# Attention steps in pairs in a two-layer gMLP and differential-attention trunk on one Trainium2 core

## What is computed

```
h  = rms_norm(x, pre_mix_g[l]);  z = h @ w_in[l]          # 1024 -> 2560: u | v | q | k | values
# A: gMLP: layer_norm(gelu(v)), per 128-position block and channel group W_s @ v + b, times gelu(u)
# B: differential attention, 4 heads, blocks of 128 queries, chunk mask:
s  = einsum('bqhjd,bkhjd->jbhqk', q, k)                    # j = 0, 1, 64 channels each
p  = softmax(where(mask, s, -1e30));  a = p[0] - lam * p[1]
o  = einsum('bhqk,bkhe->bqhe', a, v);  o = rms_norm(o, subln_g) * (1 - lam_init)
x  = x + rms_norm(concat(A, B) @ w_out[l], post_mix_g[l])
x  = x + rms_norm(swiglu(rms_norm(x, pre_ffn_g[l])), post_ffn_g[l])
```

## Time and profile before

| | us |
|---|---|
| median of 3 runs | 1099.1 |
| lowest and highest | 1099.06, 1099.11 |
| the profiled execution | 1099.09 |
| its span, first to last instruction | 1097.3 |
| PE busy | 1088.6 |
| DVE, ACT, POOL busy | 585.7, 578.5, 573.4 |

### The profile page before, as it was taken

One profiled execution on the slowest core, in us unless ns is written; L12 is line 12 of the kernel. 1 busy time (PEld: TensorE's weight loads), 2 busy tenths in 40 slices (PEclk: granted clock), 3 DMA queues, 4 the chain that ended last, 5 costly groups with the idle time before them and its releaser, 6 DMA issues.

```text
span 1097.3 us, 17449 instructions
## 1 busy us (share of the span) xinstructions
PE 1088.6 (99%) x6776; PEld 964.2 (88%) x6776; DVE 585.7 (53%) x994; ACT 578.5 (53%) x1135; POOL 573.4 (52%) x450
## 2 busy tenths in 40 slices
PE   8999999999999999999999999999999999999998
PEld 7777778999999999888887787789999999998886
DVE  4353535888888885010254445548888888820103
ACT  5656584566555554221456557756565555531212
POOL 3524254666666665544444324645776666655440
PEclk9999999999999999999999999999999999999999
DMA  8423213414334334622243221133333433353212
GB/s 278 135 58 96 67 50 96 154 57 129 94 108 116 100 95 154 210 96 96 77 136 120 77 72 64 60 95 129 101 114 95 116 114 92 105 211 116 97 57 77
DMA packets 144791, 118.33 MB, mean 108 GB/s; under 512 B 3754, under 2 KB 120004, under 8 KB 144708
## 3 DMA queue, kind: packets, MB, share of 16 engines
q1 hardware_dynamic: 144692, 117.20, 34.2%
q10 hardware_dynamic: 16, 0.00, 0.0%
HBM read 110.90 MB, written 6.29 MB: 107 GB/s over the span
## 4 chain that ended last, share of the span: by engine, by line
PE 97%; ACT 1%; DVE 1%; DMA 0%; issue 0%; DVEq 0%; ACTq 0%
PE banks L596 30%; PE banks L598 30%; PE banks L597 29%; PE banks L655 2%; PE banks L685 2%; PE banks L605 1%; PE banks L670 1%; PE banks L699 1%; PE banks L865 1%; DMA v_att<-in_pre_mix_g_dram 0%; PE banks L706 0%; ACT swap L1218 0%; PE banks L844 0%; PE banks L951 0%; ACT junk L1085 0%
## 5 line engine op out<-in xcount | busy, mean ns | idle before, releaser
L527 POOL TENSOR_TENSOR w_lo<-raw,w_hi 128x512 fp32r<-128x512 f32 x204 | 259.7, 1297 | 302.6 <-ACT w_hi L1077 302.6
L545 POOL TENSOR_TENSOR w_lo<-raw,w_hi 128x512 fp32r<-128x512 f32 x200 | 260.0, 1311 | 142.8 <-ACT w_hi L1146 138.3
L596 PE MATMUL banks<-xg_hi,w_hi 128*128 128x256 f32 (+1 forms) x896 | 278.1, 310 | 0.1
L598 PE MATMUL banks<-xg_lo,w_hi 128*128 128x256 f32 (+1 forms) x896 | 274.4, 306 | 0.0
L597 PE MATMUL banks<-xg_hi,w_lo 128*128 128x256 f32 (+1 forms) x896 | 274.0, 306 | 0.0
L1077 ACT ACTIVATE w_hi<-raw 128x1024 fp32r<-128x1024 f32 x102 | 106.9, 1056 | 170.8 <-PE banks L598 155.0
L1146 ACT ACTIVATE w_hi<-raw 128x512 fp32r<-128x512 f32 x200 | 124.9, 630 | 112.0 <-DVE raw L1761 60.7
L596 PEld LDWEIGHTS banks<-xg_hi,w_hi 128*128 128x128 f32 x896 | 171.2, 191 | 10.8 <-issue 3.3
L598 PEld LDWEIGHTS banks<-xg_lo,w_hi 128*128 128x128 f32 x896 | 171.2, 191 | 8.1
L597 PEld LDWEIGHTS banks<-xg_hi,w_lo 128*128 128x128 f32 x896 | 171.3, 191 | 6.6
L596 PE MATMUL banks<-w_hi,hid_hi 128*128 128x512 f32 x352 | 137.2, 390 | 0.0
(11 more groups left out here) (173 smaller groups left out, 1789.8 us busy)
## 6 DMA issues: line engine op xcount, KB each, us to landing
raw<-in_w_gate_up_dram SPq DMA_DIRECT2D x88, 512.0 KB, 4.1
raw<-in_w_down_dram SPq DMA_DIRECT2D x44, 512.0 KB, 3.5
raw<-in_w_in_dram SPq DMA_DIRECT2D x40, 512.0 KB, 3.8
raw<-in_w_out_dram SPq DMA_DIRECT2D x16, 512.0 KB, 3.5
x_spill<-x_rows SPq DMA_DIRECT2D x8, 512.0 KB, 5.3
x_rows<-x_spill SPq DMA_DIRECT2D x8, 512.0 KB, 5.1
x_rows<-in_x_dram SPq DMA_DIRECT2D x4, 512.0 KB, 6.8
out_dram<-x_rows SPq DMA_DIRECT2D x8, 256.0 KB, 2.0
```

The source lines that it names most:

```text
L527: last = tt(lo[:, piece], raw_half(l, c, h)[:, piece], hi[:, piece].bitcast(F32), ALU.subtract)
L545: tt(lo, full, hi.bitcast(F32), ALU.subtract).then_inc(w_ready, 1)
L596: mm(o, stat[0], mov[0], start=first, stop=False)
L598: return mm(o, stat[0], mov[1], start=False, stop=last)
```

## The change

The order of the attention part is written anew on PE, ACT and DVE.

- Scores are made two steps at a time (`scores_of_two`), without a projection between them. Maxima and combinations follow in pairs as well.
- A head's first two turned tiles go into one bank: step n % 4 = 0 at tile 0, step n % 4 = 1 at tiles 1 and 2. The second turn no longer waits for a copy of the first, and one copy of 384 columns takes both. There are 12 copies in a layer and no longer 16.
- The four gates stand in a row, in banks 2 to 5, which are the scores' banks (`GATE_BANKS`). Scores 8 and 9 wait for them to be read.
- At the start of the program the first norm's gain is loaded into rows that nothing clears, so that its DMA waits for nothing, and DVE copies it into place. Row 3 of x is normalized on DVE before the low part of row 2 is made; ACT makes the high part of row 2 after the root of row 3.

No large product is added or left out. The core of the diff:

```
+                elif n == 8 or n == 9:
+                    pe.wait_ge(gm_added, G * l + 2 * (n - 7))            # in scores
...
-                elif n == 6:
-                    pe.wait_ge(gm_added, G * l + 1)
-                elif n == 8:
-                    pe.wait_ge(gm_added, G * l + 4)
-                else:
+                elif n % ST != 1:
                     pe.wait_ge(at_copied, NS * l + n)                    # in turn
+                at = 1 if n % ST == 1 else 0
                 for k in range(n % ST + 1):
-                    last = tr(b_tr[T_BANK][:, k, :], attn[n % 2][:, k * P:(k + 1) * P], ident[:, :])
+                    last = tr(b_tr[T_BANK][:, at + k, :], attn[n % 2][:, k * P:(k + 1) * P], ident[:, :])
...
+                pe.wait_ge(a_ready, NS * l + (7 if g < 2 else 8))        # in gate
+                    last = mm(b_tr[GATE_BANKS[g]][:, n, :], v_gate[:, n, g * P:(g + 1) * P], wsT[:, g, :],
...
-            act.wait_ge(gain0_zero, 1)
-            act.dma_start(gain0_rows[0:KT, :], pre_mix_g[0].rearrange("(k p) -> k p", k=KT)).then_inc(gain0_landed, 16)
+            act.dma_start(gain0_in, pre_mix_g[0].rearrange("(k p) -> k p", k=KT)).then_inc(gain0_landed, 16)
...
+            copy(gain0_rows[0:KT, :], gain0_in).then_inc(gain0_placed, 1)
...
             norm_row(0, 2)
+            norm_row(0, 3)
             xg_low(0, 2)
-            norm_row(0, 3)
             xg_low(0, 3)
```

More of the change, by code:

```diff
@@ L954, in _ @@
+                turn_two(4)
                 weigh(l, 0)
                 va(C_VA + 1, 1, (2, 3))
-                turn(l, 4)
                 qk_half(l, 4, lower)
-                scores(l, 6)
-                turn(l, 5)
+                turn(l, 6)
                 weigh(l, 1)
                 qk_half(l, 4, upper)
-                scores(l, 7)
-                gate(l, 0)
+                turn(l, 7)
+                weigh(l, 2)
                 qk_half(l, 5, lower)
-                turn(l, 6)
-                weigh(l, 2)
@@ L967, in _ @@
                 qk_half(l, 5, upper)
-                turn(l, 7)
+                for g in range(G):
+                    gate(l, g)
+                weigh(l, 3)
                 qk_half(l, 6, lower)
-                gate(l, 1)
                 qk_half(l, 6, upper)
-                scores(l, 8)
-                gate(l, 2)
-                weigh(l, 3)
+                scores_of_two(8)
                 qk_half(l, 7, lower)
-                scores(l, 9)
-                gate(l, 3)
                 qk_half(l, 7, upper)
+                scores_of_two(10)
@@ L979, in _ @@
+                turn_two(8)
                 u_half(l, 0, lower)
-                turn(l, 8)
-                scores(l, 10)
                 u_half(l, 0, upper)
-                turn(l, 9)
-                scores(l, 11)
-                u_half(l, 1, lower)
                 turn(l, 10)
                 weigh(l, 4)
-                scores(l, 12)
+                u_half(l, 1, lower)
+                turn(l, 11)
+                scores_of_two(12)
                 u_half(l, 1, upper)
-                scores(l, 13)
@@ L991, in _ @@
-                turn(l, 11)
                 u_half(l, 2, lower)
-                turn(l, 12)
+                scores_of_two(14)
+                turn_two(12)
                 weigh(l, 5)
                 u_half(l, 2, upper)
-                scores(l, 14)
-                turn(l, 13)
                 u_half(l, 3, lower)
-                scores(l, 15)
+                turn(l, 14)
                 weigh(l, 6)
                 u_half(l, 3, upper)
-                turn(l, 14)
+                turn(l, 15)
@@ L1003, in _ @@
                 out_k(l, 0)
-                turn(l, 15)
                 out_k(l, 1)
@@ L1236, in copy_turned @@
                         act.wait_ge(pv_ready, 8 * l + (n - 4) // 2 + 1)
-                    w = (n % ST + 1) * P
-                    fn(attnT[:, AT_AT[n % ST]:AT_AT[n % ST] + w], bank[T_BANK][:, 0:w], ACT.Copy)\
-                        .then_inc(at_copied, 1)
+                    if n % ST == 1:
+                        fn(attnT[:, 0:3 * P], bank[T_BANK][:, 0:3 * P], ACT.Copy).then_inc(at_copied, 2)
+                    else:
+                        w = (n % ST + 1) * P
+                        fn(attnT[:, AT_AT[n % ST]:AT_AT[n % ST] + w], bank[T_BANK][:, 0:w], ACT.Copy)\
+                            .then_inc(at_copied, 1)
                 def take_heads(m):
@@ L1652, in _ @@
                     dve.wait_ge(par_ready, 1 + 2 * L)
-                maxima(0)
                 dve.wait_ge(ln_root_ready, l + 1)
```

140 lines of the change are left out of this document (68 added, 72 removed).

## The result

The changed kernel takes **1089.9 us** (median of 4 runs, 1089.69 to 1090.42) where the kernel before takes 1099.08 (4 runs, 1099.01 to 1099.11). The ratio is 0.9918, with a 95% interval from 0.9906 to 0.9929: 9.2 us are gone. The prediction was 1095.2, with a range from 1094.3 to 1096.8. The direction was right; the gain is more than twice what was predicted and lies outside the range.

What follows compares the result with a forecast made beforehand. PE was taken to bound the kernel. Savings of 2.9 (score pairs), 0.5 (row 3), 0.3 (rotation of q) and 0.2 (gain's DMA) sum to 3.9 us: 1099.1 to 1095.2 us, range 1094.3 to 1096.8.

Steps and rivals of the forecast that it cites:

- What bounds the kernel: Whole kernel: PE is 97% of the chain, so only its start-to-start distances and few waits count.
- Eight entries and exits a layer: Attention scores: pairing leaves eight entries and exits where 16 were, saving 1.47 us a layer, 2.9 us in two.
- Failed step 1: Joint between a pair's two scores: the second score follows like a second pass, at no extra cost.
- the other end: Eight joints of scores: each costs 0.1 us less than nothing, 1.5 us more in all; named but not taken.
- I count the rest as zero: Attention's turns and gates: fewer copies and fewer borders between fp32 and projections, beyond the scores' own, save nothing.
- Failed step 2: Program start: the gain's DMA goes some 0.3 us earlier, worth 0.2 us; bounds 0.2 lost to 0.8 gained.
- Row 3 and the rotation of q: PE's waits before row 3's turning and before layer 0's first scores go, saving 0.5 and 0.3 us.
- The covers: Attention handoffs: no new PE waits; closest are scores 10 and 11, cover 1.0 to 1.2 us, and out_k(2), 0.2.
- Joints at full or half cost: Rivals at score joints: a second score pays entry and exit fully, 1098.1 us (chance 0.06), or half, 1096.7 (0.03).
- the late end: Rival at the attention's end: ACT's chain late, PE waits 0.5 us in each layer, 1096.2 us; chance 0.11.
- starved scores: Rival in the attention: bursts from pairs make PE wait at four places a layer, 8 us lost, 1103.2; chance 0.03.

Runs made afterwards that it cites:

- the run of the pairs alone: The changed kernel with both start edits (gain's DMA and row 3) undone, leaving only the new attention order: 1091.91 us, ratio 0.9937 to the kernel before.
- the late gain: The kernel before with the gain's DMA into its own rows and DVE's copy, but its issue again waiting for the clearing: 1099.43 us, ratio 1.0003.

## Why the prediction was wrong, point by point

**What bounds the kernel: right.** PE is 98% of the chain, and everything gained was gained in its distances and gaps.

**Eight entries and exits a layer: right in kind and size.** Entry is 0.32 against 0.23 (0.31 at the pair shown) and the first step behind a pair 0.34, once per pair. This part was the predicted 1.47 us a layer.

**Failed step 1: "A score's second pass is to its first what a second score is to the first, so I take no extra cost".** A second score costs less than a first. A score's keys cost 0.213 us for 128, and 0.21 more is paid once at the ends of a run of scores, however many scores are in it (1, 2 or 4 in the runs). The two passes of a lone score carry 0.1 each of it, being the first and the last; I took that spare distance for part of the work of every pass. The prediction even named the other end, 0.1 us less at each joint, and dropped it as something "which nothing in the rows supports"; the rows did support it, and twice as much. The prediction itself says 0.63 us for 256 keys (56.63 to 57.26) and 0.21 more for each 128 keys: 0.63 - 2 x 0.21 leaves 0.21 that no key accounts for. The worth is 0.2 x 16 = 3.2 us. With the predicted 2.9 that makes 6.1; measured are 7.0 in the traces, and 6.8 in the run of the pairs alone (7.1 less the rotation's 0.3).

**A second term was put at zero: "I count the rest as zero", said of the borders with turns and gates.** These borders leave a tail. Worked out from the single starts of PE's matmuls in both layers of both kernels, the 2nd to 11th projection matmul behind any border are 0.230 us from start to start on average, those further on 0.2267, whatever they multiply. The unbroken rows of projections fall from 27 to 18 in a layer: 9 x 10 x 0.003 = 0.3 us a layer, or somewhat over 0.5 in two. The last 0.3 to 0.4 of the 7.0 I have not placed.

The page "TensorEngine Tiling (Array Packing)" of the Trainium skill, section Key Properties, was cited for the rule that a change of tiling mode drains TensorE and a change of tile does not. The traces agree that two neighbouring 64-row scores do not pay what an entry and an exit cost. They add what the rule does not give: a size, 0.35 us for each parting by a transposition, of which only 0.15 lies outside the scores' own time.

**Failed step 2: the gain's DMA, taken at 0.2 with 0.8 as the upper bound.** The start edit is worth 1.2 us in the runs and 1.4 in the trace, beyond the bound. The bound's condition came true (it landed early, 2.2 us), but what it was priced at was missing the larger part. I treated PE's time up to the turning as fixed, 4.88 to 7.68, and only moved it. It shrank, since PE, with no gap behind it, runs the same instructions up to twice as densely. The run with three idle-filling matmuls gets 1.0 us without any earlier data, the run that opens a 0.64 us gap in the changed kernel loses 0.9 of it.

**Row 3 and the rotation of q: right.** 0.5 and 0.3 us; both waits are gone and nothing was late next. 0.3 more in the same stretch had no term.

**The covers: right where named.** Scores 10 and 11 do not wait. out_k(2) starts at 157.25:

```profile
157.25 0.48 PE L600 MATMUL banks<-w_hi,ya_hi 128*128 128x512 f32 x1
```

and POOL makes the third low part from 155.81 in half of 2.59 us, ready at 157.1, a cover of 0.15 where 0.2 was worked out:

```profile
155.81 2.59 POOL L542 TENSOR_TENSOR ya_lo<-uT,ya_hi 128x512 fp32r<-128x512 f32 x2
```

**The rivals: none happened.** Joints at full or half cost are excluded by the joints themselves, the late end by the cover, starved scores by PE's list of waits. The range was built from them alone, all three on the slower side, and from a bound for the DMA; no case had both terms better than taken, and the 1.5 us that the prediction named for cheaper joints was left out of it. Summed with what was measured: 7.0 + 1.4 + 0.5 + 0.3 + 0.3 = 9.5 us, the difference of the two spans.

**Still open:** what in the first and the last pass of a run of scores takes the 0.1 us each, and what slows the ten matmuls behind a border. The records give the distances and not their cause. Nor was a run of four real scores tried, which would have to find banks for their results.

## What to carry to other kernels

Before pricing instructions that become neighbours, plot the same instruction at several sizes: what is left at size zero is a fixed cost, and neighbours may share it. At the very start of a program a gap on TensorE can cost more than itself (here one of 0.64 us cost 0.9), so look at whether equal instructions run at equal distances before and after it; work of no use that fills the gap may be faster than nothing. And when one step is moved, go through the covers behind it on every engine, not only the closest ones of the order it came from.

## What the runs showed of the hardware

- **Runs of 64-row fp32 matmuls share a fixed cost.** 0.21 to 0.23 us for a run of one, two or four scores (0.42 for 128 keys alone; 0.86 for 384 keys in two scores; 1.51 for 768 keys in four). With entry 0.09 and exit 0.05 to 0.10, an isolated score costs 0.35 to 0.4 us more than one that stands beside another. The two matmuls of a score, on different 64 rows, start 0.007 us apart and run side by side.
- **Projections speed up in an unbroken row.** 0.230 us from start to start for the 2nd to 11th matmul behind a border, 0.2267 from the 12th on, in both kernels.
- **PE's speed at the start hangs on a gap.** Twelve equal fp32 spreadings took 2.77 us behind gaps of 0.64, 1.16 and 1.53 us (the run with two matmuls on ones, the kernel before, the late gain), 2.41 and 1.88 with no gap. The distances of these instructions halve, from 0.21 to 0.11 us, between 4.1 and 6.9 us in nine traces without a gap and between 8.6 and some 11 us in five with one. A factor of two is that between the levels of 1.2 and 2.4 GHz, but the granted clock of the windows reads 1.00 on both sides of it, so here only the distances show it.
- **A small DMA at the start.** 8 x 128 numbers land 1.5 to 2.2 us after their issue at 0.73 us, and 3.85 us after an issue at 1.03, with the loads of x issued from 0.74 on. Why is not shown.
